# Sample stage with ten page-set buffers, recent keys first and softmax steps between key steps; bias rows in four copies; compression keys stored by residue

## The chip, the cores and the metric

The kernel runs on one core of one Trainium2 chip. The metric is the time of one execution on the device in microseconds, lower being better. Three executions of the kernel before gave 2705.25, 2705.33 and 2711.46; their median is 2705.33.

## The reference

One decoding step of a two-layer hybrid trunk with D_MODEL = 2048, for 512 prompt tokens and 8 samples (one new token each, with 512 tokens behind them), all in float32 with shared weights:

```python
h = rms_norm(x, g_norm[0]) * (1 + scale) + shift       # layer 0: multi-scale pooling
x = x + gate * pool_mixer(h, ...)                      # windows 2, 4, 8, 16
k_cmp, v_cmp, k_slc, v_slc, k_win, v_win = rms_norm(x, g_kv) @ w_kv
kc = silu(blocks32(k_cmp + pe) @ w_c1) @ w_c2          # blocks of 32 rows, stride 16; vc alike
h = rms_norm(x, g_norm[1]) * (1 + scale) + shift       # layer 1: three attention branches
q, z, gates = split(h @ w_in_b)
o_cmp, p = attend(q, kc, vc)                           # 31 compressed keys
o_slc = attend(q, k_slc[top 8 blocks of 64 by p], v_slc)
o_win = attend(q, k_win, v_win)                        # last 512 keys
x = x + gate * (sum(gates * o * silu(z)) @ w_out_b)
y = rms_norm(x, g_final)
```

There are 16 heads of 128 in 4 K/V groups, and every score gets a relative-position bias. For the samples the selected keys and values lie in pages of 128 rows (256 KB each) named by a page table, four pages per sample; the recent ones lie in state buffers of 512 rows (1 MB per sample). With nine blocks, of which eight are kept, one block per group is dropped.

## The kernel before, in words

One program drives five engines, each with its own instruction stream, joined by semaphores. Large projections are made of blocks of 256 output columns (Q_ numbers a block's weights, D_ its accumulators). A block has four weight tiles of 512 KB. SP loads one into RAW[j] (`load`), ACT makes its high part (`hi`, L921), DVE the low part (`lo`, L1259), and TensorE adds three products of high and low parts per tile (`quad`, `products`, L1898) to four PSUM banks D. Order in each engine is written out by hand; in `looped` bodies the splitting runs one tile ahead (`ahead`).

**Shared K/V projection** (Q_KV, twelve blocks, six tensors of two). `kv_out` (DVE, L1543) scales the accumulators by the inverse norm; TensorE turns the result (L1991), DVE copies it to one of four row buffers TM (L1564), and POOL stores it (`kv_rows`, L797). Beside these stores POOL issues, one per stored tile: in the first tiles, DRAM-to-DRAM copies of 1 MB of window state (L791), and for the tiles 16 to 23 `sample_bias`, eight copies for each sample: four of bias rows for the samples (`bd_scr`, L775) and four of every sixteenth element (`bcd_scr`, L776).

**Prompt compression.** SP loads the weights W1P over RAW, HI and LO (L574) when the projection is done with them. TensorE multiplies 32 row offsets for keys and again for values (`hidden`, L1819), reading K and V with a step of 16 columns. Meanwhile DVE, ACT and POOL normalise layer 1 (`apply(1)`, L1386, L1391, L1003, L1008), which waits for the last row copies. Then comes the gate block (Q_G), whose padding DVE clears (L1405).

**Heads.** Eight turns of a loop, each projecting q and z for two heads between scores, softmax and values of the prompt (L2042, L2059, L2073). POOL loads each turn's data.

**Sample stage.** Each sample's queries are spread over 128 rows with zeros for the other samples (QPAD, POOL L885), so the scores of all samples add up in one bank. Per sample, selected keys first and then recent ones, TensorE turns four pages for four groups (`turn_pages`, L1807) through two PSUM banks, which DVE (L1335) and ACT (L968) copy to RT_T, and multiplies (L2118, L2120, and L2124 for compressed keys). The banks are opened and closed by products with zeros (L2095, L2130). SP loads pages into four buffers PG (`page_loads`, L565, which reads four page numbers first, L562; `state_load`, L637), starting when the heads are done; for values (L2170) it reuses them. Between keys and values the three softmaxes run one after another (DVE L1665 to L1715, ACT L1240). Value weights are masked per sample by POOL (L902). After the values the branches are joined (L1728, L1730), POOL brings the residual back (L906, `s_xb`), and both ACT and DVE wait for it before they split any further weight tile.

**Output block** (Q_OB, eight blocks): product, residual and square sums (L1502, L1507), then final norm, turns and stores.

The waits around the page buffers before:

```python
sp.wait_ge(w_used, 4 * Q_OB)
sp.wait_ge(c_done, 48)
...
free = 64 + 4 * (8 * br + b) - 12
```

## Time and profile before

| | us |
|---|---|
| median of three runs | 2705.33 |
| the profiled execution | 2703.42 |
| its span | 2701.6 |
| TensorE busy | 2542.1 (94%) |
| DVE busy | 896.3 (33%) |
| ACT busy | 750.1 (28%) |
| POOL busy | 422.2 (16%) |
| share of the last chain on TensorE, DMA, DVE | 85%, 6%, 4% |
| mean granted TensorE clock | 0.965 |

The span runs from the first to the last instruction of one profiled execution. The last chain is followed back from the last instruction, at each step to what released it. The granted clock is the share of TensorE's full clock of 2.4 GHz that it was given; 0.5 is 1.2 GHz. Idle time of an engine off the chain costs nothing. TensorE records of these products come two per matmul instruction.

### The profile page before, as it was taken

What the parts mean: (1) busy time and instruction counts of PE and PEld (TensorE: products, weight loads), DVE (VectorE), ACT (ScalarE), POOL (GpSimd) and SP (SyncE); (2) the same over time, 40 slices, a digit from 0 to 9 for tenths busy, and PEclk for the clock granted to TensorE, in tenths of its full rate; (3) what the DMA queues carried; (4) which work ended last, traced back from release to release, by engine and by line L of the source; (5) the groups of instructions that cost most, each with busy time, mean ns of one, the idle gap of its engine ahead of it and who ended that gap; (6) DMA issues with size and microseconds to landing.
All of it is one profiled execution on the core that took longest, in us unless ns stands there. A gap on an engine that the chain in (4) does not pass through costs nothing.

```text
span 2701.6 us, 49851 instructions
## 1 busy us (share of the span) xinstructions
PE 2542.1 (94%) x20936; PEld 2349.6 (87%) x20936; DVE 896.3 (33%) x1560; ACT 750.1 (28%) x1266; POOL 422.2 (16%) x577
## 2 busy tenths in 40 slices
PE   7998999999999999968899999999999999876996
PEld 6987888988999999968899898989899999655996
DVE  1235112221633533322433324242433333332334
ACT  1124111112422411111432324333333333221223
POOL 1002000950000000332311112020202011111000
PEclk9998999999999999989899999999999999987998
DMA  9986776766454365699523232323222232466221
GB/s 322 330 280 220 234 228 197 227 215 216 157 154 140 126 218 180 166 79 113 119 63 89 63 89 66 90 61 92 80 76 82 71 88 64 157 210 247 94 93 64
DMA packets 321990, 395.72 MB, mean 146 GB/s; under 512 B 24846, under 2 KB 283166, under 8 KB 319906
## 3 DMA queue, kind: packets, MB, share of 16 engines
q1 hardware_dynamic: 301650, 327.66, 40.8%
q0 software_dynamic: 20144, 65.12, 8.6%
q8 instruction: 164, 2.69, 0.4%
q14 instruction: 32, 0.26, 0.0%
HBM read 372.03 MB, written 43.72 MB: 154 GB/s over the span
## 4 chain that ended last, share of the span: by engine, by line
PE 85%; DMA 6%; DVE 4%; issue 2%; ACT 2%; SPq 1%; POOL 0%; DVEq 0%; ACTq 0%; POOLq 0%
PE acc L1898 64%; PE work L1819 4%; DMA raw<-in_w_kv 3%; PE out_acc L2073 3%; PE work L1766 2%; PE work L2042 2%; PE work L1807 2%; PE work L2059 1%; PE acc L1766 1%; PE work L2036 1%; PE work L2035 1%; SPq L565 1%; PE out_acc L2070 1%; DMA ada<-in_w_ada 1%; DVE normed L1386 1%
## 5 line engine op out<-in xcount | busy, mean ns | idle before, releaser
L1898 PE MATMUL acc<-h_hi,w_hi 128*128 128x260 f32 x4896 | 1017.1, 289 | 53.8 <-DVE w_lo L1259 42.4
L1898 PE MATMUL acc<-h_hi,w_lo 128*128 128x260 f32 x4896 | 995.5, 285 | 0.0
L1898 PE MATMUL acc<-h_lo,w_hi 128*128 128x260 f32 x4896 | 994.3, 285 | 0.0
L1898 PEld LDWEIGHTS acc<-h_hi,w_hi 128*128 128x128 f32 x4896 | 764.1, 191 | 95.1 <-issue 57.8
L1259 DVE TENSOR_TENSOR w_lo<-raw,w_hi 128x1024 fp32r<-128x1024 f32 (+1 forms) x316 | 403.6, 1278 | 1134.4 <-ACT w_hi L921 1129.6
L1898 PEld LDWEIGHTS acc<-h_hi,w_lo 128*128 128x128 f32 x4896 | 764.8, 191 | 0.0
L1898 PEld LDWEIGHTS acc<-h_lo,w_hi 128*128 128x128 f32 x4896 | 763.7, 191 | 0.0
L921 ACT ACTIVATE w_hi<-raw 128x1024 fp32r<-128x1024 f32 (+1 forms) x316 | 332.5, 1053 | 1209.3 <-PE acc L1898 1147.2
L861 POOL TENSOR_TENSOR probs<-probs,row_stats 128x128 f32<-128x128 f32 (+3 forms) x128 | 111.0, 898 | 475.5 <-DVE row_stats L1612 475.5
L1819 PE MATMUL work<-rows_T_early,w_c_early 128*128 128x124 f32 x960 | 111.9, 275 | 0.7 <-ACT rows_T_early L965 0.7
L1819 PEld LDWEIGHTS work<-rows_T_early,w_c_early 128*128 128x128 f32 x960 | 109.5, 192 | 1.1 <-DVE rows_T_early L1332 1.1
L1170 ACT ACTIVATE probs<-probs,row_stats 128x128 f32<-128x128 f32 (+3 forms) x128 | 70.5, 552 | 70.0 <-DVE row_stats L1601 70.0
L2073 PE MATMUL out_acc<-probs_T,v_group 128*128 128x512 f32 (+3 forms) x256 | 76.0, 440 | 0.6
L1766 PE MATMUL work<-ada,c_cols 128*32 128x256 f32 x1024 | 70.0, 391 | 6.1 <-DMA ada<-in_w_ada 3.5
L2073 PEld LDWEIGHTS out_acc<-probs_T,v_group 128*128 128x128 f32 x256 | 46.1, 189 | 29.5 <-issue 18.4
L797 POOL DMA_DIRECT2D out<-token_rows x30 | 16.7, 556 | 273.8 <-DVE token_rows L1564 273.8
L1624 DVE COPY probs_T<-work 128x512 f32<-128x512 f32 x32 | 22.1, 692 | 106.9 <-PE work L2059 106.9
L1598 DVE CUSTOM_DVE_ANT_0 probs<-work,bias_heads 128x128 f32<-128x128 f32 (+3 forms) x128 | 55.0, 486 | 0.0
L1807 PE MATMUL work<-consts,pages_early 128*128 128x128 f32 x256 | 37.4, 294 | 17.7 <-DMA pages_early<-in_cache_k_cmp 12.3
L1206 ACT ACTIVATE z_silu<-acc 128x260 f32<-128x260 f32 x96 | 31.7, 381 | 78.5 <-PE acc L1898 78.5
L854 POOL TENSOR_TENSOR probs<-probs,row_stats 128x124 f32<-128x124 f32 x16 | 6.3, 391 | 299.0 <-DVE row_stats L1616 299.0
L1807 PE MATMUL work<-consts,pages 128*128 128x128 f32 x256 | 38.5, 298 | 14.0 <-DMA pages<-in_cache_k_slc 8.1
(319 smaller groups left out, 2010.3 us busy)
## 6 DMA issues: line engine op xcount, KB each, us to landing
ada<-in_w_ada SPq DMA_DIRECT2D x192, 512.0 KB, 4.8
raw<-in_w_in_b SPq DMA_DIRECT2D x128, 512.0 KB, 3.9
raw<-in_w_in_a SPq DMA_DIRECT2D x64, 512.0 KB, 5.0
raw<-in_w_kv SPq DMA_DIRECT2D x48, 512.0 KB, 5.0
raw<-in_w_out_a SPq DMA_DIRECT2D x32, 512.0 KB, 3.6
raw<-in_w_out_b SPq DMA_DIRECT2D x32, 512.0 KB, 3.3
x_scr<-x POOLq DMA_DIRECT2D x2, 4160.0 KB, 14.4
pages_early<-in_cache_k_cmp SPq DMA_DIRECT2D x32, 256.0 KB, 4.1
```

The costliest lines, as they stand in the source:

```text
L861: last = nc.gpsimd.tensor_tensor(PR[:, at:at + w], PR[:, at:at + w], STAT[:, 8 + t:9 + t].broadcast_to([P, w]), ALU.mult)
L921: nc.scalar.activation(HI[j % 2][:, :, 0:n], RAW[j][:, :, 0:n], ACT.Copy).then_inc(hi_ready, 1)
L1170: last = nc.scalar.activation(PR[:, at:at + w], PR[:, at:at + w], ACT.Exp, bias=STAT[:, t:t + 1], accum_out=STAT[:, 4 + t:5 + t])
L1206: nc.scalar.activation(ZB[:, blk - 1, mm, half * HT:(half + 1) * HT], D[2 * mm + half][:, 0:HT], ACT.Silu)
L1259: V.tensor_tensor(LO[j % 2][:, :, 0:n], RAW[j][:, :, 0:n], HI[j % 2][:, :, 0:n].bitcast(F32), ALU.subtract).then_inc(lo_ready, 1)
L1598: last = V.tensor_tensor_reduce(PR[:, at:at + w], where[t], BH[:, hh, (3 - t) * P:512], 1.0, -3e38, ALU.add, ALU.max, STAT[:, t:t + 1])
L1766: last = mm_((D[2], D[3], S[2])[min(s, 2)][32 * g:32 * g + 32, 256 * half:256 * half + 256], CTF[:, k, :], ADA[b][:, g, :], start=(k == 0) ...
L1807: last = tr(S[g % 2][:, P * t:P * t + P], pg[:, t, P * g:P * g + P], ident)
L1819: last = mm_((S[2] if bank == 2 else D[3])[:, 0:NKV * NCMP], w1[kv][:, l, :], at, start=(l == 0), stop=(l == CL - 1))
L1898: last = mm_(out[half][0:n, 0:HT], part[slot][:, kk, cols_], src[:, k, half * HT:(half + 1) * HT], start=(first and part is HI and src is ...
L2042: last = mm_(where[t], qs(t), kt_[:, :, 0:P * (t + 1)].rearrange("p o t -> p (o t)"), start=True, stop=True)
L2073: last = mm_(O[:, P * j:512], VG[:, br - 1, j, :], PT[:, at:at + 512 - P * j], start=(j == 0), stop=(j == 3), skip_group_check=True)
```

## The change

- The 64 bias copies become four, issued once before the pooling layer's output block. The compressed bias is read from the same rows with a step.
- K and V for compression are stored by residue (row offset first), so `hidden` reads contiguous columns; `kv_out` writes them in five pieces for the first two tensors, and the stores to DRAM are permuted.
- `apply(1)` starts under the last projection block: its writes wait per quarter for TensorE, the last `kv_out` and row copies lie inside it, W1P comes in quarters, and SP issues the last five row stores.
- Ten set buffers of 1 MB replace four: three in the operand h, two in the weight buffers, four in x, one beside. SP reads all 32 page numbers once and loads 32 sets in the order recent keys, selected keys, recent values, selected values; the first five wait only for parts of the last heads block.
- Page turns go through three PSUM banks; new and compressed keys are read in place; banks are opened by the first product, so that no zero products are needed.
- The compressed and recent softmaxes lie between the key steps of the selected branch, the selected one between value steps.
- The first output weight tiles are split during the last value steps, the others between operand tiles, and only DVE's first residual step waits for the residual.

```diff
+        SETS = [page_halves(f"set_h{i}", h_at + n * quarter, h_at + n * quarter + half_set) for i, n in enumerate((0, 4, 5))]
+        SETS += [page_halves(f"set_w{i}", BASE + 4 * 4096 + 4096 * i, BASE + 6 * 4096 + 4096 * i) for i in range(2)]
+        SETS += [page_halves(f"set_x{i}", x_at + 2 * half_set * i, x_at + 2 * half_set * i + half_set) for i in range(4)]
+        SETS += [page_halves("set_c", c_at + TS * P * 4, c_at + TS * P * 4 + half_set)]
...
+        def set_at(n):
+            parts = lambda m: 2 if m // TS % 2 == 0 else NPG
+            return n % NSET, 16 * sum(parts(m) for m in range(n % NSET, n + 1, NSET))
+        def set_page(n, t):
+            return SETS[n % NSET][t // 2][:, t % 2, :]
...
-            sp.wait_ge(lo_ready, 4 * Q_G)
-            w_c1(W1P, 0, s_cwp)
+            for j in range(4):
+                sp.wait_ge(lo_ready, 4 * (Q_G - 1) + j + 1)
+                w_c1(W1P, 0, s_cwp, j, 4)
+            sp.wait_ge(w_used, 4 * Q_G - 1)
+            w_c1(W1P, 1, s_cwp, 0, 4)
+            w_c1(W1P, 1, s_cwp, 2, 4)
             sp.wait_ge(w_used, 4 * Q_G)
-            w_c1(W1P, 1, s_cwp)
+            w_c1(W1P, 1, s_cwp, 1, 4)
+            w_c1(W1P, 1, s_cwp, 3, 4)
+            for n in range(25, 30):
+                sp.wait_ge(tm_ready, n + 1)
+                rows = P if n < 29 else TS
+                dst = kv_out_p[5][(n - 25) * P:(n - 24) * P] if n < 29 else kv_out_s[5]
+                sp.dma_start(dst, TM[n % 4][0:rows, :]).then_inc(tm_last[min(n - 25, 1)], 16)
             sp.wait_ge(cw1, 17)
             for j in range(4):
...
+            page_of = [[sp.value_load(PTAB[0:1, bass.ds(b * NPG + t, 1)], min_val=0, max_val=A["cache_k_slc"].shape[0] - 1)
+                        for t in range(NPG)] for b in range(TS)]
+            def sample_set(n):
+                i, b, kind = n % NSET, n % TS, n // TS
+                if n < 5:
+                    sp.wait_ge(w_used, 4 * (Q_OB - 1) + (1, 1, 2, 3, 4)[n])
+                elif n < NSET:
+                    sp.wait_ge(c_done, 48)
+                    sp.wait_ge(s_hd, 1)
+                elif n - NSET < 2 * TS:
+                    sp.wait_ge(ctr, 64 + 4 * (n - NSET + 1))
+                else:
+                    sp.wait_ge(pv, n - NSET - 2 * TS + 1)
+                if kind % 2 == 0:
+                    rows = A[("state_k_win", "state_v_win")[kind // 2]][b].rearrange("(t p) g d -> p t (g d)", p=P)
+                    for h in range(2):
+                        sp.dma_start(SETS[i][h][:, :, :], rows[:, 2 * h:2 * h + 2, :]).then_inc(s_set[i], 16)
+                else:
+                    cache = A[("cache_k_slc", "cache_v_slc")[kind // 2]]
+                    for t in range(NPG):
+                        sp.dma_start(set_page(n, t), cache[bass.ds(page_of[b][t], 1)].rearrange("o t g d -> (o t) (g d)")).then_inc(s_set[i], 16)
...
+            first = lambda j: load(Q_OB, j, cols(w_ob, j, 0))
+            first(0)
+            first(1)
+            sample_set(0)
+            sample_set(1)
+            first(2)
+            sample_set(2)
+            first(3)
+            for n in range(3, 4 * TS):
+                sample_set(n)
             quads(Q_OB, w_ob, 8, first=1)
...
-            def sample_bias(b):
-                for g in range(NKV):
-                    r = 32 * g + 4 * b
-                    pool.dma_start(bd_scr[r:r + 4, :], g_scr[4 * g:4 * g + 4, 0:513]).then_inc(s_bds, 16)
-                    pool.dma_start(bcd_scr[r:r + 4, :], g_scr[4 * g:4 * g + 4, 31:31 + 16 * NCMP:16],
-                                   allow_slow_non_contiguous=True).then_inc(s_bds, 16)
...
+            for g in range(NKV):
+                at = 4 * g * 2 * GLEN
+                pool.dma_start(bass.AP(tensor=bd_scr.tensor, offset=32 * g * 513, ap=[[4 * 513, TS], [513, REP], [1, 513]]),
+                               bass.AP(tensor=g_scr.tensor, offset=at, ap=[[0, TS], [2 * GLEN, REP], [1, 513]])).then_inc(s_bds, 16)
...
+                    if i < 2 and t < NT:
+                        dst = kv_out_p[i].rearrange("(n l) c -> l n c", l=CS_)[4 * t:4 * t + 4]
...
+            pool.wait_ge(s_bds, 16 * NKV)
             pool.dma_start(BD[:, :], bd_scr).then_inc(s_bd, 16)
-            pool.dma_start(BCD[:, :], bcd_scr).then_inc(s_bd, 16)
...
+                if n == 2:
+                    pool.wait_ge(s_hd, 1)
+                    for br in range(2):
+                        pool.dma_start(VN[br][:, :], kv_out_s[3 + 2 * br]).then_inc(s_vn[br], 16)
...
+                        if a == 1:
+                            act.wait_ge(w_used, 4 * (Q_G - 1) + (k - 1) // 4 + 1)
                         nc.scalar.activation(HH[:, k - 1, :], HF[(k - 1) % 3][:, :], ACT.Copy).then_inc(hhi_ready, 1)
...
+                    if a == 1 and k == 2:
+                        hi(Q_G - 1, 3)
...
             apply(1)
-            act.wait_ge(cw1, 18)
+            hidden(16, 0, CSILP)
+            hidden(17, 1, CSILP, 3)
             act.wait_ge(s_gz, 1)
             hi(Q_G, 0)
...
+            nc.scalar.activation(STAT[:, 14:15], CON[:, 0:1], ACT.Exp)
...
+            act.wait_ge(pv, 9)
+            hi(Q_OB, 0)
+            hi(Q_OB, 1)
             act.wait_ge(ydec, 1)
-            for k in range(KT):
+            for k in range(12):
                 y_hi(1, k)
-            act.wait_ge(s_xb, 16)
+            hi(Q_OB, 2)
+            for k in range(12, KT):
+                y_hi(1, k)
+            hi(Q_OB, 3)
             resid_pairs(2, Q_OB, True)
...
+                    if a == 1 and k == 2:
+                        lo(Q_G - 1, 3)
+                    if a == 1 and k == 7:
+                        kv_out(5, 1, VF)
+                        for n in range(25, 29):
+                            token_rows(n)
+                    if a == 1 and k == 13:
+                        token_rows(29)
...
+                        row = dst[:, 2 * pp + mm, :]
+                        if i >= 2:
+                            last = V.tensor_tensor(row[:, at], D[2 * mm + half][:, 0:HT], RSTD[:, at], ALU.mult)
+                            continue
+                        for a, b in (((0, 256), (256, 260)), ((260, 272), (272, TP), (TP, T)))[half]:
+                            got, rs = D[2 * mm + half][:, a - half * HT:b - half * HT], RSTD[:, a:b]
+                            if a >= TP:
+                                to = row[:, a:b]
+                            else:
+                                to = row[:, 0:TP].rearrange("p (l n) -> p l n", l=CS_)
+                                to = to[:, a % CS_:a % CS_ + min(b - a, CS_), a // CS_:(b - 1) // CS_ + 1]
+                                to = to.rearrange("p l n -> p n l")
+                                shape = "p (n l) -> p n l"
+                                got, rs = got.rearrange(shape, l=min(b - a, CS_)), rs.rearrange(shape, l=min(b - a, CS_))
+                            last = V.tensor_tensor(to, got, rs, ALU.mult)
                     last.then_inc(acc_free, 1)
...
             apply(1)
+            dve.wait_ge(cw1, 17)
+            for j in range(4):
+                last = V.memset(RAW[j][:, :, 48:P], 0.0)
+            last.then_inc(s_gz, 1)
+            compress_out(16)
             lo(Q_G, 0)
             for q, j in ahead(Q_G):
                 lo(q, j)
+                if j == 1:
+                    compress_out(17)
...
+            looped(dve, o, 8, heads, 1, 1)
+            V.memset(STAT[:, 15:16], 0.0).then_inc(s_hd, 1)
+            dve.wait_ge(s_bd, 16 * 2)
             dve.wait_ge(s_dm, 1)
...
+            for n in range(2 * TS):
+                rows_out(n)
+                if n == 8:
+                    compressed(0)
+                if n == 9:
+                    compressed(1)
+                if n == 10:
+                    masked(1)
+                if n == 11:
+                    compressed(2)
+                    greatest(1)
+                if n == 12:
+                    compressed(3)
+                if n == 13:
+                    weights(1)
+                if n == 14:
+                    compressed(4)
+                if n == 15:
+                    weights_turned(1)
+            dve.wait_ge(dsc, 2 * TS)
+            masked(0)
+            greatest(0)
+            compressed(5)
+            weights(0)
+            weights_turned(0)
...
+            o(V.tensor_tensor(yd, OD[:, :, :].rearrange("p b h -> p h b"), SZD[:, 0, :, :], ALU.mult))
+            for br in (1, 0):
+                dve.wait_ge(pv, TS * (2 - br))
                 V.tensor_copy(ACC[br][:, :], D[br][:, 0:P]).then_inc(sd_ev, 1)
...
+            for k in range(12):
                 y_lo(1, k)
-            dve.wait_ge(s_xb, 16)
+            lo(Q_OB, 2)
+            for k in range(12, KT):
+                y_lo(1, k)
+            lo(Q_OB, 3)
             looped(dve, o, 8, resid(1, Q_OB, D_OB), 2, 1)
...
+            pe.wait_ge(s_cwp[0], 64)
+            hidden(16, 0, KCF, W1P)
+            pe.wait_ge(s_cwp[1], 64)
+            hidden(17, 1, VCF, W1P, True, 3)
...
+            def turn_set(n):
+                buf, full = set_at(n)
+                pe.wait_ge(s_set[buf], full)
+                for g in range(NKV):
+                    if 4 * n + g >= 3:
+                        m, before = divmod(4 * n + g - 3, NKV)
+                        pe.wait_ge(ctre[before % 2], 32 + 2 * m + before // 2 + 1)
+                    for t in range(NPG):
+                        last = tr(S[(4 * n + g) % 3][:, P * t:P * t + P], set_page(n, t)[:, P * g:P * g + P], ident)
+                    last.then_inc(ctr, 1)
...
+            def scores_set(n):
+                br, b = 1 - n // TS, n % TS
+                q, begin, end = QPAD[n % 2], b == 0, b == TS - 1
+                pe.wait_ge(qp_ready, n + 1)
+                for c in ctre:
+                    pe.wait_ge(c, 32 + 2 * n + 2)
...
+                last.then_inc(dsc, 1)
...
+                if n == 9:
+                    pe.wait_ge(sd_ev, 1)
+                    tr(D[3][0:NKV * NCMP, P:2 * P], PX[:, :], ident).then_inc(sd_pe, 1)
...
+                elif n == 14:
+                    pe.wait_ge(sd_ev, 6)
+                    pe.wait_ge(s_cin[1], 16)
+                    for b in range(TS):
+                        last = mm_(D[3][:, NH * b:NH * b + NH], VCS[:, b, :], PTG[:, :].rearrange("p (g n) -> p g n", g=NKV)[:, :, 4 * b:4 * b + 4],
+                                   start=True, stop=True)
+                    last.then_inc(sd_pe, 1)
+            pe.wait_ge(s_cin[0], 16)
+            turn_set(0)
+            for n in range(2 * TS):
+                if n + 1 < 2 * TS:
+                    turn_set(n + 1)
+                if n == TS:
+                    pe.wait_ge(s_hd, 1)
+                scores_set(n)
+                beside(n)
...
+                pe.wait_ge(s_set[buf], full)
+                pe.wait_ge(pp_ready, m + 1)
+                for t in range(NPG):
+                    for g in range(NKV):
+                        last = mm_(D[br][rows[g], 0:P], PPAD[m % 2][:, t, rows[g]], set_page(2 * TS + m, t)[:, P * g:P * g + P],
+                                   start=False, stop=(b == TS - 1 and t == NPG - 1), skip_group_check=True)
+                last.then_inc(pv, 1)
+                if m == 3:
+                    pe.wait_ge(sd_ev, 9)
+                    weights_turn(0)
+                if m == 9 or m == 15:
+                    i = int(m == 15)
+                    pe.wait_ge(sd_ev, 11 + i)
+                    tr(S[2][:, P * i:P * i + P], ACC[1 - i][:, :], ident).then_inc(sd_pe, 1)
```

In `beside(n)` the turned and small products of the compressed softmax follow key steps 9, 11 and 12, the recent weights are turned after 13, and the products with the compressed values follow 14. `masked`, `greatest`, `weights` and `compressed(part)` hold the same DVE instructions as before.

## Rows read from the trace of the kernel before

**Rows 1.** The chain that ended last, 1000 to 1400 us: start, us, what
```profile
1078.89 0.04 DVE k_slc_T L1543
...
1129.36 0.04 DVE v_T L1543
...
1147.77 45.18 DMA raw<-in_w_kv
...
1203.83 0.04 DVE k_win_T L1543
...
1265.63 0.04 DVE v_T L1543
...
1305.31 13.89 PE acc L1898 x96
```

**Rows 2.** Who TensorE waited for, 1060 to 1340 us: total, times, longest
```profile
PE acc L1898 <- DVE w_lo L1259: 30.5, 4, 11.5
```

**Rows 3.** DMA issues, 1060 to 1140 us, then two of 1140 to 1200 us
```profile
raw<-in_w_kv SPq DMA_DIRECT2D x12, 512.0 KB, 3.6
...
raw<-in_w_kv SPq DMA_DIRECT2D x7, 512.0 KB, 25.9
...
bcd_scr<-g_scr POOLq DMA_DIRECT2D x15, 0.5 KB, 24.5
```

**Rows 4.** TensorE's timeline, compression, early and at the prompt: start, us
```profile
108.70 4.63 PE L1819 MATMUL work<-rows_T_early,w_c_early 128*128 128x124 f32 x40
...
1269.77 13.77 PE L1819 MATMUL work<-k_cmp_T,w_c_prompt 128*128 128x124 f32 x64
```

**Rows 5.** DVE's timeline, the norm of the second layer
```profile
1281.95 0.70 DVE L1386 TENSOR_TENSOR normed<-x,rstd 128x520 f32<-128x520 f32 x1
...
1284.67 0.70 DVE L1386 TENSOR_TENSOR normed<-x,rstd 128x520 f32<-128x520 f32 x1
```

**Rows 6.** The chain that ended last, 2300 us to the end
```profile
2321.44 2.17 PE out_acc L2073 x8
...
2482.02 181.49 PE acc L1898 x1488
...
2663.54 0.49 DVE x L1502
```

**Rows 7.** TensorE's timeline, sample stage
```profile
2341.50 1.09 PE L1807 MATMUL work<-consts,pages 128*128 128x128 f32 x8
...
2345.09 1.09 PE L1807 MATMUL work<-consts,pages 128*128 128x128 f32 x8
...
2374.27 1.09 PE L1807 MATMUL work<-consts,pages 128*128 128x128 f32 x8
...
2377.76 1.09 PE L1807 MATMUL work<-consts,pages 128*128 128x128 f32 x8
...
2379.20 1.09 PE L1807 MATMUL work<-consts,pages 128*128 128x128 f32 x8 [0.35 <-DVE rows_T L1335]
...
2413.62 3.43 PE L2148 MATMUL out_acc<-probs_T_cmp_gated,vc_sample 124*128 124x16 f32 x16
...
2448.52 1.08 PE L2170 MATMUL acc<-pages,probs_T_one_sample 128*32 128x128 f32 x32 [1.48 <-DMA pages<-in_state_v_win]
...
2451.08 1.93 PE L2170 MATMUL acc<-pages,probs_T_one_sample 128*32 128x128 f32 x32 [1.48 <-DMA pages<-in_state_v_win]
...
2469.44 0.77 PE L1898 MATMUL acc<-h_hi,w_hi 128*128 128x260 f32 x2 [5.85 <-issue]
```

**Rows 8.** POOL's timeline, two masked weight tiles
```profile
2423.32 2.21 POOL L902 TENSOR_TENSOR probs_T_one_sample<-probs_T_sample,consts 128x512 f32<-128x512 f32 x2 [0.26 <-PE acc L2170]
```

**Rows 9.** Issues on SP's queue, the selected keys' pages
```profile
2326.07 32.78 SPq L565 DMA_DIRECT2D pages<-in_cache_k_slc  x32
```

**Rows 10.** Key steps, value steps: us, busy PE PEld DVE ACT POOL, clock, DMA
```profile
2367.00:2396.20 29.20, 26.22 (x281) 17.52 (x281) 11.06 (x16) 11.51 (x25) 3.41 (x7) 1.00 0.86 296
...
2418.20:2443.00 24.80, 14.85 (x264) 11.59 (x260) 0.27 (x1) 0.00 (x0) 8.77 (x8) 0.57 0.72 232
```

More of the change, by code:

```diff
@@ L453, in build @@
         tm_out = [sem(f"token_rows_out{i}") for i in range(4)]
+        tm_last = [sem(f"last_token_rows_out{i}") for i in range(2)]
         s_copy = sem("states_copied")
@@ L800, in _ @@
             pool.dma_start(x_scr, flat(X[:, :, :])).then_inc(s_xs, 16)
-            for i in range(6):
+            for i in range(5):
                 kv_rows(i)
@@ L905, in _ @@
+            for m in range(2 * TS):
+                br = 1 - m // TS
+                pool.wait_ge(sd_ev, 7 if br else 10)
+                wait(pool, pv, m - 1)
+                split = lambda x: x[:, :, :].rearrange("p t (g b r) -> p (t g) b r", g=NKV, b=TS)
+                nc.gpsimd.tensor_tensor(split(PPAD[m % 2]), split(PTD[br]), mask(m % TS).broadcast_to([P, NPG * NKV, TS, REP]), ALU.mult).then_inc(pp_ready, 1)
             pool.wait_ge(ydec, 1)
@@ new lines, in scores_set @@
+            def scores_set(n):
[4 more added lines that the diff above has]
+                    pe.wait_ge(c, 32 + 2 * n + 2)
+                rows = [slice(32 * g, 32 * g + 32) for g in range(NKV)]
+                for g in range(NKV):
+                    mm_(D[br][rows[g], :], q[:, g, :], RT_T[n % 2][:, g, :], start=begin, stop=end, skip_group_check=True)
+                for g in range(NKV):
+                    last = mm_((O, D[2])[br][rows[g], 0:1], q[:, g, :], (KS, KW)[br][:, g, TP + b:TP + b + 1],
+                               start=begin, stop=end, skip_group_check=True)
+                if br:
+                    for g in range(NKV):
+                        last = mm_(D[3][rows[g], 0:NCMP], q[:, g, :], KCS[:, b, NCMP * g:NCMP * g + NCMP],
+                                   start=begin, stop=end, skip_group_check=True)
+                last.then_inc(dsc, 1)
```

426 lines of the change are left out of this document (154 added, 272 removed).

## The prediction

> **What bounds the kernel now.** I read the page first. TensorE is busy for 94% of the span and the chain that ended last is 85% TensorE, so time is won only where TensorE waits or does work that goes away. I then took the waits of TensorE, stage by stage, and the chain in order of time.
>
> The first place is the shared K/V projection. Each of its six parts ends with a DVE step that scales the last accumulator, and the chain shows those moments [rows 1]: 1078.89, 1129.36, 1203.83 and 1265.63 us. The part that ends at 1129.36 took 50.47 us, the next two took 74.47 and 61.80. The excess is 24.0 + 11.3 = 35.3 us. The waits of TensorE say what it is: 30.5 us on the low half of a weight tile [rows 2], and the chain has one weight load of 45.18 us in it [rows 1]. The DMA views [rows 3] give the cause's neighbour: while the small bias copies (0.5 KB each, 24.5 us to landing) are in the queues, a 512 KB weight load takes 25.9 us, and 3.6 us in the stretch before, where whole megabytes of window state are copied.
>
> The second place is the stretch from the last accumulator of the projection (1265.63) to the first product of the gate block (1305.31), 39.7 us. TensorE works most of it, but on compression products of 13.77 us per 64 records [rows 4], where the early ones, which read their rows by residue, take 4.63 us for 40, so 7.4 for 64. DVE applies the norm only then, at 2.72 us per two of the sixteen tiles [rows 5].
>
> The third is the sample stage, from the end of the heads (2321.44 + 2.17 = 2323.61) to the first product of the output block (2469.44), 145.8 us [rows 6, 7]. There TensorE turns and scores at 3.5 us per sample, waits for pages, stands still during the softmax, and multiplies values at the pace of the transfers. Behind it the output block has a hole up to 2482.02, where the second weight tile waited for the residual to come back.
>
> **Part 1, bias copies.** 64 copies on POOL's queue go, 32 of them of single elements; four copies with the same rows of 2052 bytes come, issued before the output block of the pooling layer, and BD's strided columns take the place of the second table. POOL's issue time was beside TensorE's work, so I price it at nothing. The wait it caused is worth 35.3 us. The bounds are 0 (the token rows, also in flight, were the cause) and 35.3; I take all of it, because the parts with megabyte copies and token rows but no bias copies show no such wait [rows 1, 3]. The four new copies meet weight loads earlier: 0 to 4 us, I take 0, as the rows of 2 KB of other tables are written there too.
>
> **Part 2, keys by residue, norm moved up.** The kept scaling step becomes five instructions instead of two for the first two parts. It is exposed once in each part; I add 0.45 us each, 0.9 us (0 to 4, were the strided writes slow). So the projection gains 34.4.
>
> The norm of the second layer now starts under the last projection block. Its first tiles wait for the quarter of the product operand that TensorE has left, and DVE reaches the last scaling step at its eighth tile. What is left after the accumulator: scaling and four token-row copies 4.3 us (4.1 before, from 1265.63 to 1269.77 [rows 1, 4], and the longer wait for the second copy), then ten more turns at 1.36 us [rows 5] and the drain, 14.5 us, then about 2.2 for clearing the gate padding, a copy and a low half, six instructions of 0.3 to 0.7 us: 21.0. TensorE's own path: transposes 4.3, two compressions at 7.4 [rows 4], and 2.5 to 3.5 for the second products and the copies between them: 21.8 to 22.8. I take 22.5 against 39.7, a gain of 17.2. The prompt weights are loaded in quarters behind the last weight tiles; their second half is issued at the accumulator's end and is wanted 11 us later. Cover gone, it costs up to 5. The last five row stores move past the weight loads on SP's queue, and the gate weights stand behind them; these are wanted at about +19 and can be issued at about +13. Bounds of the gain 9 to 20.
>
> **Part 3, sample stage.** Key steps: 3.59 us with compressed scores and 3.49 without (differences of starts in [rows 7]), each with a 0.35 us wait on a copy that a third bank removes. 8 x 3.24 + 8 x 3.14 = 51.0. The zero products go. Beside the later steps TensorE still does the eight products with compressed values, 3.3 [rows 7], and some transposes and small products, about 3: 6.3. DVE's softmax instructions lie between its copies, where it has some 1.2 us per step free; two of the parts are longer or wait for TensorE: 2 us. The first copy waits for the bias load, which POOL issues when the heads' products end, and which then meets the fourth and fifth sets: 1 us (0 to 6). Values: TensorE needs 1.08 for a sample, POOL 2.21 for two masks [rows 8], so POOL sets about 1.18: 18.9, and 1.7 for the new rows and the turned weights. The selected softmax starts after the last score and is wanted after four value steps (4.7 us against some 4.6 of DVE and ACT): nothing, or 2. Tail: a copy and a turn 0.7, then idle time, 5.85 before [rows 7], now 4.5 as one branch is already in. Sum 51.0 + 6.3 + 3.0 + 20.6 + 5.2 = 86.1, a gain of 59.7.
>
> This needs the transfers to keep up. A window set of 1 MB lands every 2.56 us [rows 7]. Five sets are in, or under way, when the heads end; the rest run ahead of a reader at 3.2 us per set until the tenth buffer. At the end of the keys nine or ten value sets are in, the last six follow at 2.56 from about +63, the last at about +79, wanted at +80. It is just covered. SP reads 32 page numbers before the first set: some 18 us, behind the last head load, where only weights for later stand behind it.
>
> A rule speaks against this sum. The Trainium skill ("DMA: Bandwidth & Descriptors", Specifications) puts one core's share of HBM at about 358 GB/s; by it a set would take 2.9 us, an estimate, and the sample stage would end some 2 us later. The trace does not agree: it shows a megabyte every 2.56 us.
>
> **Part 4, output block.** It took 2663.54 - 2469.44 = 194.1 [rows 6, 7]. Now the first two weight tiles are split during the last value steps, the others between operand tiles, and only the residual step waits for the residual, which has 25 us of products over it. 1488 records took 181.49, so 1536 take 187.3: a gain of 6.8 (bounds 2 and 8).
>
> **Sum.** 34.4 + 17.2 + 59.7 + 6.8 = 118.1. The profiled execution took 2703.42 (span 2701.6), which gives 2585.3; it is 1.9 below the median of the three runs, 2705.33, so I say 2586.
>
> **Rivals.**
> A, the forecast: 2571 to 2604.
> B, the bias copies were bystanders, and the weight loads still crawl in the fifth and sixth parts. For it: token rows are also in the queue there. Against: they are in the earlier parts too. 2586 + 35 = 2621.
> C, transfers bind the sample stage. SP issued and landed the four 256 KB pages of a set in 32.78 / 8 = 4.1 us [rows 9], half of that reading page numbers, which is gone. If pages still need 4.1, the transfers after the fifth set take 11 x 2.56 + 16 x 4.1 = 93.8, the last set lands near +96 and the output block starts at +102: 16 us more, 2602. The Trainium skill ("DMA: Bandwidth & Descriptors", Bandwidth) has a rule on this side: batch transfers to a megabyte or more for 75% of peak, which the pages are not.
> D, the clock. In the value steps of before, with waits between them, TensorE's granted clock was 0.57, and in the key steps 1.00 [rows 10]; a sample's value products then took 1.93 instead of 1.08 [rows 7]. That is 1.2 in place of 2.4 GHz for much of that stretch. If the small products are at half clock throughout, the keys cost (51.0 + 6.3) x (1.93 / 1.08 - 1) = 45 more and the values 16 x 0.8 = 13: 2644. Against it: the waits go.
> E, slower than before. The place is the set transfers in the sample stage, ten in flight with weights and residual beside them. They slow each other as the weight loads were slowed in [rows 3]. The other parts give 58.4, the stage may last 145.8 + 58.4 = 204.2 before the kernel is slower, so it decides from (204.2 - 2) / 27 = 7.5 us per set. 25.9 us for 512 KB speaks for the possibility, 2.56 per megabyte with several in flight against it. At 8 us per set: 2719.
>
> **Chances.** A 0.68, B 0.08, C 0.16, D 0.06, E 0.02. The range holds A and C, with the bounds of the unknown costs: 2570 to 2612. Within 0.3% (8 us, about what a measurement of this kernel can tell from no change) 0.01, faster 0.97, slower 0.02.
>
> **What would show it.** Right: the six projection parts end 50.5 us apart and no weight load lands after more than 10 us; gate products start 22 us after the last scaling step; compression products take 7.4; key steps 3.1 to 3.3 with no wait on a set; value steps 1.2; first output product 86 us after the heads; no hole after it. Wrong, if a set is what value or key steps wait for (C), if the granted clock in the sample stage is below 0.9 (D), if weight loads of the fifth part still land after 20 us (B), or if DVE's copies, behind its softmax instructions, stop the key steps for more than 5 us in all.

## The result and the profile after

| | before | changed |
|---|---|---|
| median, us | 2705.29 | 2583.82 (2579.59 to 2591.25, four runs) |
| ratio | | 0.9549, 95% interval 0.9522 to 0.9577 |
| profiled span, us | 2701.6 | 2577.8 |
| TensorE busy, us | 2542.1 | 2487.6 |
| mean granted TensorE clock | 0.965 | 0.987 |

The forecast was 2586, in a range of 2570 to 2612. The span of the profiled execution fell by 123.8 us, where 118.1 were forecast; the medians are 121.5 us apart.

The chain that ended last, changed kernel: start, us, what.

```profile
970.44 1.16 DVE k_cmp_T L1583 x5
...
973.32 7.55 DMA out<-token_rows
...
1023.46 0.04 DVE v_cmp_T L1583
...
1026.77 7.50 DMA out<-token_rows
...
1078.36 0.04 DVE k_slc_T L1570
...
1128.83 0.04 DVE v_T L1570
...
1179.31 0.04 DVE k_win_T L1570
...
1229.77 0.04 DVE v_T L1570
...
1234.08 7.14 PE work L1922 x64
1241.22 7.15 PE acc L1922 x64
...
1250.28 11.74 PE acc L2001 x96
```

Against [rows 1], the parts that end at 1128.83, 1179.31 and 1229.77 are 50.5 us apart, and no weight load is in the chain. The compression products take 7.15 us per 64, against 13.77 in [rows 4]. Earlier there is something new: the chain goes twice through a row store of over 7 us.

TensorE's timeline, sample stage of the changed kernel (start, us, instruction, in brackets the idle time before it and what ended it):

```profile
2263.95 2.32 PE L2176 MATMUL out_acc<-probs_T,v_group 128*128 128x512 f32 x8
2266.11 1.47 PE L2207 MATMUL work<-consts,set_h 128*128 128x128 f32 x12
2270.94 3.75 PE L2207 MATMUL work<-consts,set_h 128*128 128x128 f32 x20 [3.36 <-DVE rows_T L1718]
...
2276.00 2.17 PE L2207 MATMUL work<-consts,set_h 128*128 128x128 f32 x16
...
2279.22 2.17 PE L2207 MATMUL work<-consts,set_w 128*128 128x128 f32 x16
...
2327.49 1.08 PE L2283 MATMUL acc<-set_x,probs_T_one_sample 128*32 128x128 f32 x32 [0.58 <-POOL probs_T_one_sample L919]
...
2341.89 1.96 PE L2283 MATMUL acc<-set_x,probs_T_one_sample 128*32 128x128 f32 x56 [1.09 <-issue]
...
2353.59 0.77 PE L2001 MATMUL acc<-h_hi,w_hi 128*128 128x260 f32 x2 [4.18 <-issue]
```

Here `set_h`, `set_w`, `set_x` and `set_c` are the set buffers. The heads end at 2263.95 + 2.32 = 2266.27, the output block starts at 2353.59: 87.3 us, against 145.8 in [rows 6, 7]. Key steps start 3.22 us apart; the first copy waits, and value steps wait a little for POOL. Nothing here waits for a set. The end of the chain:

```profile
2353.59 186.37 PE acc L2001 x1536
...
2539.99 0.49 DVE x L1527
```

All 1536 records run in one piece, where [rows 6] had 1488 behind a hole. In these blocks each product has one record (eight blocks of 192); two per instruction, as the text on the profile before has it, holds for the compressions, with 64 records for 32 products.

To part the span in full, one moment of the kernel before is wanted that no row ahead shows, the first scaling step of the projection (its chain):

```profile
977.96 0.77 DVE k_cmp_T L1543 x2
```

| stretch | before | changed | gain | forecast |
|---|---|---|---|---|
| to the first scaling step | 977.96 | 970.44 | 7.5 | 0 |
| to the last one | 287.7 | 259.3 | 28.3 | 34.4 |
| to the gate products | 39.7 | 20.5 | 19.2 | 17.2 |
| to the heads' end | 1018.3 | 1016.0 | 2.3 | 0 |
| sample stage | 145.8 | 87.3 | 58.5 | 59.7 |
| output block | 194.1 | 186.4 | 7.7 | 6.8 |
| final norm and stores | 38.1 | 37.8 | 0.3 | 0 |

### The profile page after: what moved, and what is told of

It is laid out like the page before. It is cut to its first block, busy times and chain, and to the rows that moved or that the text cites. A ratio compares the mean times of both kernels' runs of the same rounds, so it can differ in the third digit from the quotient of the medians.

```text
span 2577.8 us, 49490 instructions
## 1 busy us (share of the span) xinstructions
PE 2487.6 (96%) x20912; PEld 2307.1 (89%) x20912; DVE 898.6 (35%) x1589; ACT 747.2 (29%) x1243; POOL 382.0 (15%) x510
## 4 chain that ended last, share of the span: by engine, by line
PE 90%; DVE 3%; issue 2%; DMA 2%; SPq 2%; ACT 1%; POOL 0%; DVEq 0%; ACTq 0%; POOLq 0%
PE acc L2001 68%; PE work L1922 4%; PE out_acc L2176 3%; PE work L1869 2%; PE work L2145 2%; PE work L2162 1%; PE work L2207 1%; PE acc L1869 1%; PE work L1910 1%; PE work L2139 1%; PE work L2138 1%; PE out_acc L2173 1%; PE acc L2220 1%; DMA out<-token_rows 1%; DMA ada<-in_w_ada 1%
## 5 line engine op out<-in xcount | busy, mean ns | idle before, releaser
L1910 PE MATMUL work<-consts,pages_early 128*128 128x128 f32 x256 | 36.6, 290 | 17.0 <-DMA pages_early<-in_cache_k_cmp 12.7
L1910 PEld LDWEIGHTS work<-consts,pages_early 128*128 128x128 f32 x256 | 30.6, 149 | 22.7 <-issue 17.2
L1869 PEld LDWEIGHTS work<-ada,c_cols 128*32 128x32 f32 x1024 | 26.7, 109 | 26.3 <-DMA ada<-in_w_ada 4.2
```

The source lines that it names most:

```text
L1869: last = mm_((D[2], D[3], S[2])[min(s, 2)][32 * g:32 * g + 32, 256 * half:256 * half + 256], CTF[:, k, :], ADA[b][:, g, :], start=(k == 0) ...
L1910: last = tr(S[g % 2][:, P * t:P * t + P], pg[:, t, P * g:P * g + P], ident)
```

## The experiments

All times are single profiled runs unless a ratio is given. The first scaling step of the projection (L1583 in the changed kernel) has nothing before it that the experiments edit, but for the four new copies, which two of them leave out; yet it was reached between 970.4 and 976.8 us in the changed kernel and its variants. The stretch from the gate products to the heads' end, which no experiment edits either, took 1013.0 to 1019.4 us. So terms of a few us are read from a stretch of the trace, counted from its own start. Nor are whole times compared between experiments: they ran on several chips, and single runs of the kernel before took 2700.23 us on one and 2689.45 us on another.

### Which copies crowd the queues

All 64 copies back, in place of the four:

```diff
+                    elif n < 3 * TS:
+                        for g in range(NKV):
+                            r = 32 * g + 4 * (n - 2 * TS)
+                            pool.dma_start(bd_scr[r:r + 4, :], g_scr[4 * g:4 * g + 4, 0:513]).then_inc(s_bds, 16)
+                            pool.dma_start(bcd_scr[r:r + 4, :], g_scr[4 * g:4 * g + 4, 31:31 + 16 * NCMP:16], ...
```

> The changed kernel with the 64 bias copies back beside the row stores of the tiles 16 to 23 (32 of four rows, 32 of single elements, the latter into a table that nothing reads), in place of the four. Theory (the copies slowed the weight loads): the fifth and sixth projection parts last 74.5 and 61.8 us again instead of 50.5, the loads land after 20 us or more, and the whole is some 35 us longer than the changed kernel, about 2619 us. Rival (bystanders; the reading by residue, the other loads or POOL's order freed the loads): the parts stay within 2 us of 50.5 and the time is about 2584 us.

Only the second of the two kinds, the 32 copies of single elements, added beside the four new ones:

> The changed kernel with 32 copies of single elements (four rows of every sixteenth element, 0.5 KB each) added, and the four new copies kept. Theory (single elements are what crowds the queues): nearly all of the loss of the run with all 64 comes, 25 to 35 us in the fifth and sixth parts. Rival (any 32 small transfers cost their share): about half, 15 to 18 us, here and in the run with the row copies alone. Second rival (the copies of rows do it): under 5 us here.

Only the first kind, the 32 copies of rows, in place of the four:

> The changed kernel with 32 copies of four rows of 2052 bytes in place of the four long ones. Theory (single elements are what crowds the queues): 0 to 5 us longer than the changed kernel, and the fifth and sixth parts within 2 us of 50.5 each. Rival (every small transfer costs its share): 15 to 18 us. Second rival (rows do it): 25 to 35 us.

| | fifth part | sixth part | time |
|---|---|---|---|
| before | 74.5 | 61.8 | 2703.42 |
| all 64 | 67.1 | 62.5 | 2611.92 |
| single elements | 75.7 | 57.2 | 2619.17 |
| rows | 50.5 | 50.5 | 2584.19 |
| changed | 50.5 | 50.5 | 2579.59 |

The single elements are the cause, and rows alone cost nothing in these two parts. With all 64 the two parts lose 28.6 us, with the elements alone 32.0. The windows (us, busy PE, PEld, DVE, ACT, POOL, granted clock, share of the 16 DMA engines, GB/s) show how; first the kernel before:

```profile
1130.00:1180.00 50.00, 37.76 (x309) 36.83 (x310) 12.16 (x16) 5.78 (x6) 28.08 (x45) 0.93 1.22 58
```

the same stretch with rows alone:

```profile
1130.00:1180.00 50.00, 48.61 (x402) 47.67 (x402) 15.55 (x22) 8.49 (x8) 13.02 (x25) 1.00 0.35 110
```

and with elements alone:

```profile
1130.00:1180.00 50.00, 40.56 (x331) 39.20 (x330) 12.24 (x18) 5.30 (x5) 16.83 (x25) 0.94 1.04 57
```

Its DMA view of the loads issued from 1120 to 1180 us (count, size, median us to landing; 3.5 in the changed kernel):

```profile
raw<-in_w_kv SPq DMA_DIRECT2D x7, 512.0 KB, 33.6
```

With single elements the DMA engines are shown fully taken (1.04, and 1.22 in the kernel before) while they move 57 and 58 GB/s; without them they are a third taken (0.35) and move 110. POOL's issuing is not the cause: rows alone and elements alone show the same 25 instructions of POOL, busy 13.0 and 16.8 us of the 50. The Trainium skill ("DMA: Bandwidth & Descriptors", Specifications) gives 512 bytes as the least transfer for line rate; the trace agrees, for pieces of 4 bytes.

The same number of elements in four copies instead of 32, at one place:

```diff
+                    elif n == 2 * TS:
+                        pool.wait_ge(s_bds, 16 * NKV)
+                        for g in range(NKV):
+                            pool.dma_start(bcd_scr[32 * g:32 * g + 32, :], bd_scr[32 * g:32 * g + 32, 31:512:16], ...
```

> The changed kernel with the 3968 single elements of the 32 element copies moved by four copies of 992 elements each, issued at the first row store of the fifth tensor, from the rows that the four new copies made. Theory (the cost lies in the elements, each 4 bytes of its own, whatever the number of copies): weight loads land after 20 us or more behind them and 20 to 35 us are lost in the fifth part. Rival (the cost lies in the number of copies that cross the loads): under 8 us.

Neither bound was met. Its chain:

```profile
1133.94 0.04 DVE v_T L1576
1140.99 31.54 DMA raw<-in_w_kv
1193.99 0.04 DVE k_win_T L1576
1244.45 0.04 DVE v_T L1576
```

These moments are the starts of the last scaling steps of the fourth, fifth and sixth part. One load still took 31.5 us, but the fifth part lost only 9.6 us (60.05 instead of 50.5) and the sixth nothing, against 32.0. The median weight load issued from 1120 to 1180 us landed after 11.9 us, where the 32 copies made it 33.6. So the number of elements alone does not fix the cost. Three things differ besides: the number of copies and how they are spread over time, the rows per copy (32 instead of 4, which mattered for the stores below), and the source (the copied rows, 513 elements apart). How much each counts is left open.

### The permuted stores

```diff
                         dst = kv_out_p[i].rearrange("(n l) c -> l n c", l=CS_)[4 * t:4 * t + 4]
+                        for l in range(4):
+                            pool.dma_start(dst[l], TM[n % 4][32 * l:32 * l + 32, :]).then_inc(tm_out[n % 4], 16)
+                        continue
```

> The changed kernel with each permuted row store of the first two tensors issued as four copies of 32 rows. In the changed kernel such a store lands 7.5 us after its issue, and DVE's copy into the row buffer waits for it, twice, with TensorE behind it for 4.3 us. Theory (one store whose slowest dimension is 4 is spread over a quarter of the engines that move data): four copies of 32 rows land after 2.5 to 4 us, the two waits of TensorE on the low half of a weight tile between 900 and 1030 us vanish, 4 us less there. Rival (the order of the rows in DRAM makes them slow, in whatever pieces): they still land after 7 us and the 4.3 us stay.

The DMA view of the stores issued from 900 to 1020 us (size, median us to landing), changed kernel:

```profile
out<-token_rows POOLq DMA_DIRECT2D x4, 256.0 KB, 13.0
```

and this one, where the kernel with plain stores of 256 KB (below) has 9.0:

```profile
out<-token_rows POOLq DMA_DIRECT2D x16, 64.0 KB, 6.0
```

Its chain has no store left in it:

```profile
971.36 1.16 DVE k_cmp_T L1586 x5
...
1224.48 0.04 DVE v_T L1573
```

From 971.36 to 1224.48 are 253.1 us, against 259.3: the stalls cost 6.2 us, more than the 4.3 of one group of waits, and splitting the stores removes them. The expected landing time was missed: 6.0 instead of 2.5 to 4, beside copies of a megabyte. The order of the rows in DRAM isn't the cause, as it is the same in both kernels. The Trainium skill ("DMA: Bandwidth & Descriptors", "Why a DMA increments its semaphore by 16 and not by 1") says that a transfer is spread over as many engines as divide the slowest dimension of both sides, so four for four groups of 32 rows; the runs agree with it, but no view here shows how many engines a store used.

### Keys by residue

```diff
-                        if i >= 2:
+                        if i >= 0:
...
-            hidden(16, 0, KCF, W1P)
+            hidden(16, 0, KCF, W1P, False)
```

(and the same for the values; the stores are plain again.)

> The changed kernel with the keys and values of the compression kept in their order: the scaling step is two instructions again, the stores to DRAM are plain, and the compression products read with a step of 16 columns. Theory: the two compressions take 13.7 us each instead of 7.15, so the gate products start 33 to 34 us after the last scaling step instead of 20.5 (13 us more); the two stalls of 2.2 us between 900 and 1030 us and 0.6 us of scaling go; in all 8 us more than the changed kernel. Rival (the time up to the gate block is set by the norm on DVE, and the products only fill it): the gate products start within 3 us of 20.5, and the whole is 2 to 5 us shorter than the changed kernel, as the stalls go.

Its chain:

```profile
976.20 0.77 DVE k_cmp_T L1570 x2
...
1228.56 0.04 DVE v_T L1570
...
1232.86 13.61 PE work L1922 x64
1246.47 13.60 PE acc L1922 x64
...
1261.80 11.79 PE acc L2001 x96
```

The gate products start 33.2 us after the last scaling step, 12.7 more. The projection takes 252.4 us, 7.0 less than with keys by residue: 6.2 for the stalls and 0.4 for each longer scaling step. As the change has it, the layout thus gains 12.7 - 7.0 = 5.7 us; with the stores split it would gain 11.9. Of the expected 8 us more these stretches show 5.7, as the stalls were larger than thought, and the rival fell: the norm on DVE does not set the time up to the gate products. Without the layout they still start 39.7 - 33.2 = 6.5 us sooner than in the kernel before; the norm was moved up for that, and no run parts it further.

### The transfers of the sample stage

Four buffers and no early set:

```diff
+        SETS = SETS[5:9]
...
-                if n < 5:
+                if n < 0:
```

> The changed kernel with four set buffers instead of ten, none filled before the heads end. Theory (the ten buffers and the early start keep the transfers off the path): key steps wait for sets at first (a first set 5 to 8 us after the heads), then run at the pace of the transfers where it is slower than 3.2 us, and value steps, with no sets ahead, run at 2.56 us or more each instead of 1.4: 16 x 1.2 = 19 us and the late start of 6 us, some 25 us more than the changed kernel. Rival (the transfers keep pace, and the buffers past the fourth are room that isn't needed): under 8 us more, all of it at the first set.

Ten buffers and no early set:

```diff
-                if n < 5:
+                if n < 0:
```

> The changed kernel with ten buffers, but the first five sets too wait for the end of the heads. Theory: TensorE waits 5 to 8 us for the first set, after which ten buffers run ahead; the last sets then come some 10 us later than before and the value steps wait for them: together 8 to 15 us more than the changed kernel. Rival (only the first set counts, the lead is made up during the key steps, since a set lands in 2.56 us and is read in 3.2): 5 to 8 us more, with no wait in the value steps.

Page numbers read per set, not ahead of the first:

```diff
+                    page_of = {b: [sp.value_load(PTAB[0:1, bass.ds(b * NPG + t, 1)], min_val=0, max_val=A["cache_k_slc"].shape[0] - 1)
+                                   for t in range(NPG)]}
```

> The changed kernel with the four page numbers read before each set of pages again (16 readings in 4s beside the transfers) instead of 32 before the first set. Theory (the page sets cost SP 4.1 us each when it reads their numbers, as in the kernel before, and 2.1 without): sets of pages are issued every 4.1 us, the sets for the values come late and the value steps wait for them, up to 16 us more than the changed kernel. Rival (the buffers hide it): value steps as in the changed kernel, and the first set sooner after the last load of the heads; under 3 us either way.

| | heads' end to output block | against 87.3 |
|---|---|---|
| four buffers | 2274.21 to 2382.08 = 107.9 | +20.6 |
| ten, none early | 2265.16 to 2364.84 = 99.7 | +12.4 |
| numbers per set | 2273.21 to 2378.55 = 105.3 | +18.0 |

With four buffers TensorE waits 6.8 us for the first set, where the changed kernel waits 3.4 for the bias rows, and the value steps wait (TensorE's waits, 2240 to 2420 us: total, times, longest):

```profile
PE acc L2284 <- DMA set_x<-in_cache_v_slc: 7.2, 8, 1.5
PE work L2208 <- DMA set_x<-in_state_k_win: 7.1, 2, 6.8
...
PE acc L2284 <- DMA set_x<-in_state_v_win: 4.0, 4, 2.0
```

Of the 20.6 us, 12.4 come with the late start alone, so the six further buffers are worth the other 8.2.

With the numbers per set, SP's own queue is in the chain. Its timeline:

```profile
2333.64 2.40 SPq L680 DMA_DIRECT2D set_w<-in_cache_v_slc  x4
2338.45 15.14 SPq L680 DMA_DIRECT2D set_x<-in_cache_v_slc  x16
```

These two sets of pages are 4.8 us apart, half of it (2.4) issues, the rest readings of numbers; the six that follow are 4.3 to 4.8 apart, and the value steps wait for the last sets. This is rival C of the prediction, which had 16 us for it. In the changed kernel four such sets are issued in 11.35 us, with waits for buffers among them. The clock fell too: with the waits back, the granted clock in the value steps was 0.69 with four buffers (2337 to 2377 us) and 0.70 with the numbers per set (2333 to 2374 us), where the changed kernel has 1.00 (shown below). No run parts what the clock adds from the waits themselves. A loss came in all three, 20.6 for some 25 expected, 12.4 within 8 to 15, and 18.0 where up to 16 was expected; the rivals, that the buffers or the lead were room to spare, fell.

### The hole of the output block

```diff
             act.wait_ge(pv, 9)
             hi(Q_OB, 0)
-            hi(Q_OB, 1)
...
+            act.wait_ge(s_xb, 16)
+            hi(Q_OB, 1)
```

(and the same on DVE; tiles 2 and 3 follow all operand tiles too.)

> The changed kernel with only the first weight tile of the output block split ahead of the residual's return; the tiles 1 to 3 follow the operand tiles and wait for it, as in the kernel before. Theory (that wait made the hole of the kernel before): TensorE stops for 5 to 9 us after the first tile's products, and the 1536 records from the first output product last 192 to 195 us instead of 186.4. Rival (the hole came from the order alone, and in the changed kernel the residual is back before it is wanted): under 2 us.

Its chain:

```profile
2350.00 14.49 DMA x<-x_scr
...
2366.95 181.56 PE acc L1999 x1488
```

With the first product at 2353.03 the block takes 2548.51 - 2353.03 = 195.5, 9.1 more than 186.4: the hole is back, and with it the 1488 records of [rows 6]. The chain runs from the residual's load through the split of the tile to them, so it is the wait and not the order.

### Three edits together

```diff
-            dve.wait_ge(s_bd, 16 * 2)
-            dve.wait_ge(s_dm, 1)
...
+                    dve.wait_ge(s_bd, 16 * 2)
+                    dve.wait_ge(s_dm, 1)
...
-        PPAD = [place(f"probs_T_one_sample{i}", [P, NPG, P]) for i in range(2)]
+        PPAD = [place(f"probs_T_one_sample{i}", [P, NPG, P]) for i in range(3)]
...
-                wait(pool, pv, m - 1)
+                wait(pool, pv, m - 2)
```

The third is the split of the permuted stores.

> Three edits on the changed kernel, each against a wait that its trace shows: the permuted row stores as four copies of 32 rows (4.3 us of waits went, and the time with it, in the run with that edit alone); DVE's wait for the bias rows moved from ahead of its first copy of turned keys to ahead of the softmax that needs them (3.4 us of wait at the first copy); a third buffer of masked value weights, so that POOL is one sample ahead (2.5 us of waits on POOL). Theory (each wait is all that stands there): 4.3 + 3.4 + 2.5 = 10.2 us less than the changed kernel, a ratio to the kernel before of about 0.951. Rivals: the bias wait only moves (something else is late at the first copy, so under 1 us of the 3.4 comes back), and POOL, at 1.1 us a mask, is the pace of the value steps whatever the buffers (so 1 us or less of the 2.5): 5 us less in all.

> The changed kernel itself, not edited, timed beside the others on one chip. Both theories: a ratio to the kernel before of 0.955, within 0.003.

The ratio to the kernel before is 0.9539 (0.9520 to 0.9558), median 2577.27 of five; for the changed kernel on the same chip 0.9563 (0.9543 to 0.9584), median 2581.76 of five. The medians differ by 4.5 us, not by the 10.2 of the theory, and the intervals overlap: that the three together are faster is likely, not shown by the times. The trace of the three together, TensorE's timeline around the first copy:

```profile
2264.97 2.32 PE L2182 MATMUL out_acc<-probs_T,v_group 128*128 128x512 f32 x8
...
2269.58 2.53 PE L2213 MATMUL work<-consts,set_h 128*128 128x128 f32 x20 [0.98 <-DVE rows_T L1722]
2272.05 1.07 PE L2226 MATMUL acc<-rows_T,q_one_sample 128*32 128x512 f32 x8
```

The first scores follow the heads by 2272.05 - 2267.29 = 4.8 us, where the changed kernel, run again beside it, took 8.3: 3.5 us. The part after v_cmp takes 50.9 us (1026.49 to 1077.35) instead of 54.9, and the projection 253.1 again. So two of the three waits went, with 3.5 and some 6 us, and the bias wait did not only move. Against this the stretch up to the heads' end, unedited, took 1018.0 us, where the changed kernel had 1013.1 when run again. The third buffer gave little: from the last key step to the last value product are 24.4 us, against 24.0, and 25.5 when the changed kernel was run again, so its effect is below what two traces of one kernel differ by. TensorE's waits in the sample stage say why:

```profile
PE acc L2289 <- issue: 3.5, 3, 1.9
PE acc L2289 <- POOL probs_T_one_sample L922: 1.2, 2, 1.0
```

The waits on POOL halved, from 2.5 to 1.2, but time in which TensorE waited for nothing that the profile shows was 3.5 (1.6 in the changed kernel, but 3.0 when that was run again). What that is stays open, and of the 2.5 us expected from the buffer none can be shown.

## Why the prediction was right, and where it was off

**The sum.** Forecast 118.1, measured 123.8. More than the whole excess, 7.5 us, lies ahead of the first scaling step, where variants without any edit there differ by up to 6.3 us among themselves; this is no effect of the change that I can show. It hides that the first part gave 6.1 us less than forecast. So it is partly luck that the forecast lies 2 us from the median; that the other three parts came within 2 us of their terms is not.

**Part 1.** The step "I take all of it" was right: the 35.3 us are gone, the 64 copies bring 28.6 of them again, and the element copies alone 32.0. The step "0.9 us" for the longer scaling was right as well (0.4 each). What failed is a step that the prediction did not take: it named the permuted stores in the part on the change and gave them no price. They hold DVE's row buffers, DVE's copy waits, and the splitting of the next weight tile is queued behind it: 6.2 us. So 28.3 instead of 34.4.

**Part 2.** 20.5 us after the last scaling step, 22.5 forecast. The chain runs over TensorE's own path, whose terms add up to 21.6 to 22.6 and not, as written, 21.8 to 22.8. The term "2.5 to 3.5 for the second products and the copies" was 1.9 (1248.37 to 1250.28), and the compressions took 7.15 each instead of 7.4. That the products, not the norm, set it is shown by keys in order: 12.7 us more, nearly the 12.9 that two compressions take more.

**Part 3.** 87.3 against 86.1. Key steps 3.22 and 3.13 instead of 3.24 and 3.14. Two terms were mis-sized. The bias load: 1 us taken, 3.4 measured, inside its bounds of 0 to 6; it landed after 5.05 us. The value steps: 24.0 us from the last key step to the last product, where 20.6 were forecast. POOL's 1.18 per sample was right for most, but there are waits of 0.4 to 1.0 us on it and gaps without a visible cause, and one mask took twice its time. The small products beside the keys, 6.3 taken, were 3.65 (in the chain 0.26 + 0.32 + 0.16 + 0.32 + 0.59 + 0.11 + 1.89), and the 2 us for DVE's softmax did not show: no key step after the first waits. So the keys end 58.5 us after the heads (60.3 forecast), the rest takes 28.8 (25.8), and the errors nearly cancel, which is luck too.

**Part 4.** 186.4 against 187.3; the hole is caused by the wait for the residual, as said, and is worth 9.1 us here, more than the 6.8 it was priced at.

**The rivals.** B fell: the loads are held up again when the element copies are back. C is real, with its price (18.0 against 16), where page numbers are read beside the transfers; the change avoids it by reading them all ahead. Its 4.1 us per set came from a row of issues, which doesn't show when a page has landed. D did not come: both over the key steps and over the value steps, where the kernel before had 0.57 [rows 10], the windows show a clock of 1.00.

```profile
2275.00:2320.00 45.00, 44.99 (x519) 30.90 (x511) 24.79 (x55) 17.23 (x32) 7.86 (x16) 1.00 1.05 403
...
2325.00:2349.00 24.00, 18.94 (x530) 14.39 (x526) 10.29 (x22) 2.82 (x4) 17.43 (x14) 1.00 0.88 321
```

So with the waits gone most value products take 1.08 us per sample, and none the 1.93 of [rows 7]. The first row also answers E: the set transfers, with up to ten buffers open, moved 403 GB/s, which makes 2.6 us for a set of 1 MB, and not the 7.5 from which E was reckoned. It also answers the rule that the prediction weighed: the Trainium skill ("DMA: Bandwidth & Descriptors", Specifications) has about 358 GB/s for a core, and this row shows more. The measurement decides.

## What to carry to other kernels

Look for DRAM copies of single elements near a stream of large loads, even where their issue is hidden and their bytes are few: 16 KB of them cost 32 us here. Price a store by what its buffer is waited for, and look at the shape of its slowest dimension when a change permutes it. Buffers and an early start pay only while the queue that fills them keeps up: here reading four page numbers per set took back 18 of 58 us.

## What was unexpected of the hardware

A mask of POOL takes 1.13 us [rows 8], but beside a weight tile that DVE splits, 2.1. In the changed kernel (POOL's timeline):

```profile
2340.47 2.14 POOL L919 TENSOR_TENSOR probs_T_one_sample<-probs_T_sample,consts 128x512 f32<-128x512 f32 x1 [0.25 <-PE acc L2283]
```

and DVE's, where two splits take 3.29 us:

```profile
2340.41 3.29 DVE L1282 TENSOR_TENSOR w_lo<-raw,w_hi 128x1024 fp32r<-128x1024 f32 x2
```

In the run that waits for the residual DVE splits one tile there, in 1.22 us:

```profile
2340.22 1.22 DVE L1281 TENSOR_TENSOR w_lo<-raw,w_hi 128x1024 fp32r<-128x1024 f32 x1
```

and POOL's mask, begun just behind it, still takes 2.15:

```profile
2340.28 2.15 POOL L919 TENSOR_TENSOR probs_T_one_sample<-probs_T_sample,consts 128x512 f32<-128x512 f32 x1 [0.25 <-PE acc L2281]
```

The next mask settles what the second split does. Beside it, in the changed kernel, and without it, in the run that waits (both from the chains):

```profile
2342.92 1.78 POOL probs_T_one_sample L919
```

```profile
2343.00 1.14 POOL probs_T_one_sample L919
```

So a mask is slow where a split runs beside it. The first mask seems to stand until the first split is through, and with a second split queued that one takes its turn behind: 3.29 instead of 2 x 1.22. The Trainium skill ("GPSIMD Engine Reference", Specifications) says that the two engines share their interfaces to SBUF when DVE reads two inputs from it, as a split does; the rows agree. That whole instructions take turns is read from these durations; no run tests it further.
